# Attention of a hybrid decoder trunk: the two heads of a pair in plain float32 on the two halves of the matmul array

## The reference, cut to what matters

```python
s = einsum('bqghd,bngd->bghqn', q_c, kc) * scale      # compressed keys, 31 of them
o_cmp = einsum('bghqn,bngd->bqghd', masked_softmax(s, valid), vc)
...                                                   # selected keys: with 8 blocks and top 16 all are taken
o_slc = softmax(q_c . kg, causal) . vg                # so this branch is causal attention on ks, vs
o_win = softmax(q_c . kwc, causal window 512) . vwc   # and this one on kw, vw: 512 tokens, so causal as well
return g_c[..., 0:1] * o_cmp + g_c[..., 1:2] * o_slc + g_c[..., 2:3] * o_win
```

## Time and profile before

| | |
|---|---|
| runs, median of 3 | 1786.74 us (1786.24 to 1787.28) |
| profiled execution | 1785.22 us |
| its span, first to last instruction | 1783.4 us |
| PE, DVE, ACT busy | 1764.0, 856.6, 592.8 us |
| granted TensorE clock, mean | 1.000 |
| attention, first compressed scores (L823) to last transposes | 522.9 to 627.0 us |

### The profile page before, as it was taken

How to read it: one execution, slowest core, us unless ns; L and a number is a source line. 1 busy time by engine, 2 the same in 40 slices (tenths; PEclk the granted TensorE clock), 3 DMA queues, 4 the chain that set the end, 5 groups by cost and what they waited for, 6 DMA issues and landing times.

```text
span 1783.4 us, 22116 instructions
## 1 busy us (share of the span) xinstructions
PE 1764.0 (99%) x8132; PEld 1462.5 (82%) x8132; DVE 856.6 (48%) x1100; ACT 592.8 (33%) x832; POOL 86.5 (5%) x81
## 2 busy tenths in 40 slices
PE   8999999999999999999999999999999999999999
PEld 6888888877878888888888888888888888888887
DVE  5544443347788845444443344444432554444322
ACT  5333332234336634333322233333222433333211
POOL 0500000012000010000000000000001000000000
PEclk9999999999999999999999999999999999999999
DMA  6333333352320023333343323333332233333331
GB/s 178 95 94 96 103 111 96 88 130 60 94 71 13 1 67 99 95 94 94 95 127 93 96 84 95 98 101 94 113 97 67 77 106 95 94 94 112 109 97 48
DMA packets 321362, 163.68 MB, mean 92 GB/s; under 512 B 13893, under 2 KB 320041, under 8 KB 321322
## 3 DMA queue, kind: packets, MB, share of 16 engines
q1 hardware_dynamic: 321130, 163.08, 31.9%
q10 hardware_dynamic: 192, 0.08, 0.0%
HBM read 161.04 MB, written 2.10 MB: 91 GB/s over the span
## 4 chain that ended last, share of the span: by engine, by line
PE 93%; DVE 3%; ACT 2%; issue 1%; DMA 0%; SPq 0%; POOL 0%; DVEq 0%; ACTq 0%
PE ps_s L532 20%; PE ps_s L533 20%; PE ps_s L534 20%; PE ps_y L532 9%; PE ps_y L534 9%; PE ps_y L533 9%; PE ps_aux L862 1%; DVE w_lo L1392 1%; ACT w_hi L1014 1%; DVE scratch L1404 1%; ACT scratch L1270 0%; PE ps_y L845 0%; DMA x_in<-in_x 0%; PE ps_s L813 0%; DVE small L1746 0%
## 5 line engine op out<-in xcount | busy, mean ns | idle before, releaser
L1392 DVE TENSOR_TENSOR w_lo<-raw,w_hi 128x1024 fp32r<-128x1024 f32 (+1 forms) x275 | 365.3, 1328 | 725.2 <-ACT w_hi L1014 725.0
L532 PE MATMUL ps_s<-xg_hi,w_hi 128*128 128x512 f32 x1576 | 617.9, 392 | 0.1
L534 PE MATMUL ps_s<-xg_hi,w_lo 128*128 128x512 f32 x1576 | 613.4, 389 | 0.0
L533 PE MATMUL ps_s<-xg_lo,w_hi 128*128 128x512 f32 x1576 | 613.3, 389 | 0.0
L1014 ACT CAST w_hi<-raw 128x1024 fp32r<-128x1024 f32 (+1 forms) x275 | 307.9, 1119 | 583.1 <-PE ps_y L534 291.7
L532 PEld LDWEIGHTS ps_s<-xg_hi,w_hi 128*128 128x128 f32 x1576 | 295.9, 188 | 67.1 <-DVE w_lo L1392 2.8
L533 PEld LDWEIGHTS ps_s<-xg_lo,w_hi 128*128 128x128 f32 x1576 | 295.9, 188 | 62.4 <-issue 1.7
L534 PEld LDWEIGHTS ps_s<-xg_hi,w_lo 128*128 128x128 f32 x1576 | 295.9, 188 | 61.9
L532 PE MATMUL ps_y<-act_hi,w_hi 128*128 128x512 f32 x704 | 274.3, 390 | 0.7 <-DVE w_lo L1392 0.7
L534 PE MATMUL ps_y<-act_hi,w_lo 128*128 128x512 f32 x704 | 273.9, 389 | 0.0
L533 PE MATMUL ps_y<-act_lo,w_hi 128*128 128x512 f32 x704 | 273.9, 389 | 0.0
(11 more groups left out here) (310 smaller groups left out, 1035.8 us busy)
## 6 DMA issues: line engine op xcount, KB each, us to landing
raw<-in_ffn_w_gate SPq DMA_DIRECT2D x88, 512.0 KB, 3.9
raw<-in_ffn_w_up SPq DMA_DIRECT2D x88, 512.0 KB, 3.9
raw<-in_ffn_w_down SPq DMA_DIRECT2D x64, 704.0 KB, 4.6
raw<-in_hyb_w_in SPq DMA_DIRECT2D x19, 512.0 KB, 3.8
x_in<-in_x SPq DMA_DIRECT2D x8, 256.0 KB, 6.0
w_raw<-in_hyb_cmp_w SPq DMA_DIRECT2D x4, 512.0 KB, 6.8
raw<-in_hyb_w_in SPq DMA_DIRECT2D x8, 256.0 KB, 3.8
raw<-in_hyb_w_out SPq DMA_DIRECT2D x16, 128.0 KB, 2.9
```

What stands on the lines that cost most here:

```text
L532: mm(bank, hi, x_hi, start=first, stop=False, **kw)
L533: mm(bank, hi, x_lo, start=False, stop=False, **kw)
L534: return mm(bank, lo, x_hi, start=False, stop=last, **kw)
L1392: tt(w_lo[:, n % 2, 0:size], raw[:, n % 4, 0:size], f32(w_hi[:, n % 2, 0:size]), ALU.subtract).then_inc(lo_ready, 1)
```

## The change

The scores no longer use split operands: `keys` holds the plain float32 keys, group 0 on partitions 0 to 63, group 1 on 64 to 127, and a step multiplies head j of group 0 on array rows 0 to 63 and head j of group 1 on rows 64 to 127. A step is now one branch (`s // 4`) of both heads. The values of the two heads go to partitions 0 to 63 and 64 to 127 of the output bank, each with 64 value columns. `q_parts`, `k_hi`, `k_lo`, `kc_hi`, `kc_lo` and all their casts and subtractions go. An output is split once for both heads (128 partitions, two per j) where it was split per head (64 partitions, four per j). For c = 0 and 1 ACT copies both turned banks in one instruction and DVE none. The compressed part of `values` is added at the end of the second branch. The loop over j = 1, 2 is written out.

```diff
             def scores(j, s):
...
-                pe.wait_ge(qp_lo_ready, 2 * j + g + 1)
+                if s == 0:
+                    pe.wait_ge(rope_ready, head_tiles("q3" if j == 3 else "kc"))
                 at_least(pe, exp_done, 8 * j + s - 1)
...
-                for br in range(2):
-                    bank = ps_s[:, 2 * (s % 2) + br, :]
-                    mm(bank[:, 0:wide], query, k_hi[:, br, g, 0:wide], start=False, stop=False, skip_group_check=True)
-                    last_mm = mm(bank[:, 0:wide], query, k_lo[:, br, g, 0:wide], start=False, stop=True,
-                                 skip_group_check=True)
+                for g in range(2):
+                    rows_ = slice(g * DH, (g + 1) * DH)
+                    last_mm = mm(ps_s[:, 2 * (s % 2) + g, 0:width], qf[rows_, j * T + c * P:j * T + (c + 1) * P],
+                                 keys[rows_, br, 0:width], start=False, stop=True, skip_group_check=True)
...
             def values(j, pair):
...
+                heads = [ps_aux[g * DH:(g + 1) * DH, queries] for g in range(2)]
+                def values_of(g, k):
+                    return v_t[:, br, k * P + g * DH:k * P + (g + 1) * DH]
+                if pair in (0, 3):
+                    at_least(pe, o_lo_ready, 2 * j + pair // 3)
+                for k in range(2 * half_of + 1):
+                    for g in range(2):
+                        mm(heads[g], values_of(g, k), probs[:, g, k, :, :], start=pair == 0 and k == 0, stop=False,
+                           skip_group_check=True)
...
+                if br == 1:
+                    pe.wait_ge(c_pt_ready, 2 * j + 2)
+                    for g in range(2):
+                        last_mm = mm(heads[g], vc_t[:, g * DH:(g + 1) * DH], ptc[:, g, queries], start=False, stop=True,
+                                     skip_group_check=True)
...
             def take_probs(j, s):                        # ACT
...
+                both = c < 2
+                act.wait_ge(pt_done, 16 * j + 2 * s + 1 + both)
+                last = copy(turned(pair % 2)[:, 0:1 + both, 0:c + 1, c % 2, :],
+                            ps_y[:, 0:1 + both, 0:(c + 1) * P].rearrange("p g (k q) -> p g k q", q=P))
...
             def take_probs(j, s):                        # DVE
...
+                if c < 2:
+                    return
                 dve.wait_ge(pt_done, 16 * j + 2 * s + 2)
...
-                    if s in (3, 7) and not last:
-                        query_low(j + 1, s // 4)
```

More of the change, by code:

```diff
@@ L248, in build @@
             small_c = mb("small_c", [P, 5, NQ])
-            w2_hi, w2_lo = (q_parts[:, i, 0:2 * P].rearrange("p (c d) -> p c d", c=2) for i in range(2))
+            keys_c = mb("keys_c", [P, 2 * NCP])
         with ExitStack() as pool_ctx:
@@ L892, in _ @@
             attend(0, first=True)
-            with pe.Fori(1, 3) as j:
+            for j in (1, 2):
                 attend(j)
@@ L1183, in kc_square, with take_values_c @@
                 nc.scalar.activation(kcm[:, 0, :], square_in, ACT.Square).then_inc(head_sq, 1)
[L1185 to L1189, removed]
+            def take_values_c():
                 act.wait_ge(aux_done, AUX.index("t_vc") + 1)
@@ L1268, in exps @@
                 act.wait_ge(negmax_ready, 8 * j + s + 1)
[L1269 to L1272, removed]
+                for g in range(2):
+                    last = nc.scalar.activation(prob_of(s)[:, g * T:g * T + width], ps_s[:, 2 * (s % 2) + g, 0:width],
+                                                ACT.Exp, bias=small[:, s % 2, g:g + 1],
+                                                accum_out=small[:, s % 2, 2 + g:3 + g])
                 last.then_inc(exp_done, 1)
@@ L1323, in _ @@
             attend(0, first=True)
[L1324 removed]
+            for j in (1, 2):
                 attend(j)
             attend(3, last=True)
[L1327 removed]
+            split_output(3, 0)
             take_probs(3, 7)
[L1329 removed]
+            split_output(3, 1)
             for d in range(KD):
@@ L1554, in rope @@
                 tt(dst, dst, m1[:, :], ALU.add).then_inc(rope_ready, 1)
-            def keys_low(br):
-                dve.wait_ge(k_hi_ready, br + 1)
-                for g in range(2):
-                    rows_ = slice(g * DH, (g + 1) * DH)
-                    for h in range(2):
-                        last = tt(k_lo[h * DH:(h + 1) * DH, br, g, :], work[rows_, br, :], f32(k_hi[rows_, br, g, :]),
-                                  ALU.subtract)
-                last.then_inc(k_lo_ready, 1)
             def pairs_of(n, p, c):
@@ L1607, in _ @@
             gain_and_norm("kw", R_KN + 2, work[:, 1, :])
-            rope("ks", work[:, 0, :])
+            rope("ks", keys[:, 0, :])
             split(U_MIX + 6)
@@ L1611, in _ @@
             scaled(U_MIX + 4, 4, vt[:, :])
-            rope("kw", work[:, 1, :])
+            rope("kw", keys[:, 1, :])
             split(U_LOOP)
@@ L1805, in attend @@
                         convolved_low(3, work[:, 0, :])
-                    if s % 2 == 0 and not (first and s <= 2):
-                        output_low(j, (s - 4) // 2)
+                    if s in (0, 2) and not first:
+                        output_low(j - 1, s // 2)
                     if not (first and s == 0):
```

162 lines of the change are left out of this document (51 added, 111 removed).

## The result

The changed kernel takes 1772.07 us, the median of four runs (1771.05 to 1772.36), beside 1786.68 us for the kernel before on the same chip (1786.24 to 1787.28): ratio 0.9919, 95% interval 0.9907 to 0.9932, 14.6 us faster. The forecast was 1778.3 us, faster. The sign held, and so did the mechanism, two matmuls at once on the two halves; but the order in which the forecast let them run did not, and the gain was 8.4 us on paper and 14.6 on the chip. The likeliest case's own range (1771 to 1785) just holds the time.

What follows compares the result with a forecast made beforehand. PE was taken to bound the steady half rounds, DVE the first. Terms -5.8, -1.4 and -1.2 made -8.4 us on 1785.22, 1776.8; with 1.5 us for the runs' median, 1778.3 us, range 1766 to 1801 (8 in 10).

Steps and rivals of the forecast that it cites:

- likeliest case: Whole kernel: the two array halves overlap, 1771 to 1783 us at chance 0.42; its own range 1771 to 1785.
- Rival 1: Attention scores and values: the halves don't overlap in plain float32, 1800 us; chance 0.28.
- rival 2: Attention: halves overlap but each change of form costs more, or only columns overlap, 1783 to 1793 us; chance 0.20.
- rival 3: Attention: full overlap at little cost, DVE becomes the bound at 10.0 us per half round, 1765.5 us; chance 0.10.
- (a): Scores on PE: two heads' records take three record times instead of four, 3.35 us, +0.43 per half round.
- (b): Values on PE: alternating pairs overlap, n pairs taking 2n + 1 record times, 3.0 us, -2.26 per half round.
- (c): Changes of the array's form on PE: ten row changes at 0.15, columns nothing, +1.5 us per half round; bounds 0 and 4.0.
- (d): PE's waits, mostly for DVE's copy of a turned bank: 0.75 us per half round falls to 0.25, -0.5.
- Steady half round: Attention after its first half round: PE's terms sum to -0.83 us per half round, giving 11.8 us.
- The start and the first half round: Before and in the first half round: -1.4 us from PE's 1.67 us wait, -1.2 from DVE's lighter load; bounds 0 and -2.8.
- The key splits before 520 cost nothing: Before the attention: removing the key splits before 520 us gains nothing, since PE has no gap there.
- Seven half rounds at one rate: Attention: the last half round counted like the steady ones, its last values standing in the output projection; -5.8 us in seven.

Runs made afterwards that it cites:

- both edits: Changed kernel, narrow turned banks split between ACT and DVE except in the first two steps, compressed scores issued with the next step's scores: 1768.33 us, ratio 0.9900.
- in twos: Changed kernel with the values of odd pairs in the order A A B B A B instead of alternating heads: 1771.9 us, one run.
- in threes: Changed kernel with the values of odd pairs in the order A A A B B B: 1774.27 us, one run.
- blocked: Changed kernel with all values matmuls of head A first, then all of head B: 1783.14 us, ratio 0.9985 to the kernel before.
- merged: Changed kernel with compressed scores and the next step's scores issued together, two changes of form fewer per half round: 1771.12 us, ratio 0.9919.

## Why the prediction was right, and where its sum was off

**What bounds.** PE bound the steady half rounds and DVE the first, as read. The kernel got faster because two matmuls run at once; put on one half, scores cost 1.91 us more per half round and values 2.58. Rival 1 (no overlap) is out, rival 2 (dear changes of form) too, and rival 3 (DVE binds) is not reached even in the version with both edits, at 10.5 us per half round with PE full. The forecast was right because it chose overlap against none; its 8.4 us are the sum of terms of which several were off, in both directions.

**(a) Scores: the failed size.** "Three record times instead of four", with 0.44 for the narrowest step, gave +0.43 per half round. The single records of after show head A's first at 574.189 and head B's first at 574.196, 7 ns apart, then the second ones at 574.722 and 574.729. That is two record times. Over four steps they make 2.15 us without the changes of form, 1.2 less than the forecast's 3.35. Its own sign said so too: it wanted 1.3 us for a step of 512 keys, and 1.06 were measured. The cause is the premise that B's records can only come behind both of A's. The orders in twos, in threes and blocked each show a record of the free half passing waiting ones of the busy half. The load limit of 0.11 for each record also didn't hold across halves: in the step of 128 keys the first weight loads of the two heads start at 578.041 and 578.047, the second ones at 578.149 and 578.156.

The Trainium skill (TensorE: Matmul & The Clock Gate, Part 3) says that matmuls keep program order in start and end, which the forecast had used for its three out of four. For the start the measurement decides against it: 579.83 before 579.93 in the blocked order, 571.88 before 571.99 in the merged one.

**(b) Values: near, by two errors that nearly cancel.** Forecast 3.0 us per half round, measured 2.90 on average. By compressed part and pair: 1.67 and 2.10 for an odd pair (564.13 to 565.80, 575.25 to 577.35), 0.80 and 1.23 for an even one. The forecast's chains of 2n + 1 record times rest on the same premise as (a). Here too the heads' first records start together (575.248 and 575.255), so a chain is 2n: 7 and 3 record times instead of 8 and 4, which with the compressed 0.43 is 2.58 us, 0.43 less. The other 0.3 is the price of the change to 64 columns and back, which the forecast put at nothing. That the total agreed was luck.

**(c) Changes of form: right for the rows, missed for the columns.** Forecast 1.5 for ten changes of rows. The distances give about 0.12 on the way in (0.20 where 0.08 stood) and 0.21 more than two record times from the first score to the next instruction, for each of four scores, and 0.23 for the compressed trip as the merged version shows: 4 x 0.33 + 0.23 = 1.55. The single records of the widest step show where the 0.21 lies: the second records start 0.53 behind the first (574.189 to 574.722) where a record takes 0.43, and the next instruction 0.53 behind the second. The columns were taken over from the trip into 32 output columns, which costs nothing in before. The trip into 64 does cost: the second record of an odd pair starts 0.267 behind the first instead of 0.216, and from the last one to the next full matmul it is 0.317 (577.028 to 577.345). That is 0.15 for each of two trips. Then the first transposes behind scores and values stand 0.165 apart where 0.109 is their rhythm, three times per half round: 0.17. So the changes cost 1.55 + 0.31 + 0.17 = 2.0 us, 0.5 above the forecast. Behind such a change the weight load starts only with its matmul (573.707 for 573.710, 577.342 for 577.345); these loads are the 15 waits "issue" of L838 in the list above.

**(d) Waits: little given back.** The forecast took 0.75 us of standing per half round out of the waits of PE's weight loads and gave 0.5 of it back. But a weight load is drawn ahead of the matmuls in flight (the load of the masks that start at 577.837 begins at 577.730, beside the last transpose), so its wait is no standing of the array: read in the same way, after would stand 2.9 us. PE's idle time is too small instead: (75.92 - 74.26) / 6 = 0.28 before and (67.22 - 65.34) / 6 = 0.31 after. A transpose is recorded with 0.27 us and the next one starts 0.11 behind it, so each stop loses 0.16 us in the idle time. The starts say it: 20 transposes at 0.109 are 2.18 us per half round.

| us per half round, third to seventh, from start to start | before | after |
|---|---|---|
| compressed scores with their mask | 0.93 | 1.16 |
| scores with their masks | 3.26 | 3.80 |
| values | 5.24 | 2.90 |
| transposes of the compressed probabilities | 0.43 | 0.45 |
| other transposes and what PE stands behind them | 2.77 | 2.80 |
| together | 12.63 | 11.12 |

So before stood 2.77 - 2.18 = 0.59 us, at two places. One is DVE's copy of a turned bank, on average 0.31:

```profile
579.12 0.33 PE L845 MATMUL ps_y<-consts,prob 128*128 128x128 f32 x1 [0.31 <-DVE pt_odd L1785]
```

The other, 0.28, is before the masks of the step of 256 keys. In after the first is gone, as forecast. The second has grown to 0.46, behind ACT's joint copy, which "has room" in busy time but lies ahead of an exponential in the queue. PE's own work before was 12.0 us (forecast 11.9); 0.13 was given back, not 0.5. Where the joint copy is split again, about 0.1 us remain.

**Steady half round.** -0.83 forecast, -1.51 measured in the third to seventh (-1.45 over all six). Corrected by (a) -1.2, (b) -0.43, (c) +0.5 and (d) +0.37 the forecast would be -1.6.

A sum of the prediction does not come out: with 0.5 to 2.2 us for (c) its own terms give a gain of 15.4 to 3.5 us, not 16 to 1.5. Its forecast does not use these bounds.

**The start and the first half round.** Forecast -2.6, measured -1.7. The wait of 1.67 us shrank to 0.79 only:

```profile
527.84 0.69 DVE L1517 TENSOR_TENSOR work<-ps_y,rstd 128x512 f32<-128x512 f32 x1 [0.87 <-PE ps_y L530]
528.59 0.28 PE L805 MATMUL ps_s<-mask_b,ident_b 128*128 128x128 bf16 x2 [0.79 <-DVE work L1517]
```

The DVE instruction itself now waits 0.87 us for PE's product. With the two low parts (1.4 us) gone DVE is early, and then it is PE that it waits for.

**Missed.** "The key splits before 520 cost nothing" was wrong by 0.9 us. Before had a wait of PE for ACT's square:

```profile
436.23 1.12 PE L707 MATMUL ps_stat<-scratch,consts 128*128 128x512 f32 x2 [0.39 <-ACT scratch L1151]
```

In after the same instruction has none, nor is there one for w_lo near 446 us. PE looks full there, and I took that for no gap. The later start of after is not the reason: the wait is missing in every version of it, also in the changed kernel timed again, whose PE comes to this place 0.15 us earlier than before's. That it was the key splits leaving ACT and DVE is inferred from these traces; no run put them back alone.

**The end.** Seven half rounds at one rate was the forecast's stand-in; the last one and its values into the projection gave -3.0, twice a steady one. The values of three pairs fall into it, 8.7 us before and 5.4 after.

## What to carry to other kernels

Plain float32 matmuls of 64 rows or 64 output columns ran two at once here when they stood on different halves of the array: count a pair of the same width as one, and add the changes of form, 0.33 us for a trip into 64 rows around scores and 0.15 for one into 64 columns. Alternate the two heads, or at most two matmuls of each, and don't block three. Read how long PE stands from the distances of its starts against its rhythm; the waits of its weight loads say too much (2.9 us in after), its idle time too little (0.31 where 0.46 were lost). Before moving copies to the engine with free busy time, look at what stands behind them in its queue: here it was the exponential that the bounding engine waits for.

## What the runs showed of the hardware that was not expected

- Records of two heads on different row halves start 7 ns apart (574.189 and 574.196) and cost one record time together: 1.06 us for four records of 512, against 1.91 on one half. On column halves 12 records of 256 take 1.34 us against 2.64.
- A record for the free half starts ahead of waiting ones for the busy half. Three passed ones occur (orders in twos, in threes and blocked); with four waiting, in threes and blocked, it was held. Whether the depth is a number of records or of instructions with their loads, no run here tells.
- A trip from 128 rows to 64 and back costs some 0.33 us around the scores, and 0.23 was saved where one was merged away. A trip into 64 output columns costs 0.15 (0.05 behind its first record, 0.10 before the next full matmul); one into 32 cost nothing.
- Three readings of how long PE stands per half round differ: by the waits of weight loads 0.75 us before and 2.9 after, by PE's idle time 0.28 and 0.31, by the distances of starts 0.59 and 0.46.
- With the scores of both heads on one half the granted clock fell in parts of the attention (0.79 over one half round of 16.31 us instead of 13.03), which it did in the attention of no other profiled execution here; the cause is open.
